# Attention stage of a decoder layer: the key projection's first step, two splits and a copy change places, and VectorE combines a long tile's probabilities in two parts

## The chip, the cores and the metric

The kernel runs on one core of one Trainium2 chip. The metric is the device time of one execution in microseconds (us), lower is better. TensorE multiplies, VectorE and ScalarE work on its results, GpSimd takes a few powers, SyncE and ScalarE issue the transfers.

## The reference, cut to what matters

One decoder layer over 1024 tokens of width 1024, in float32: an input projection, a chunked state scan (SSD), differential attention with four head pairs, an output projection, cross-attention into 256 memory tokens, and a squared-ReLU MLP, each with norms around it. What the change touches is above all the differential attention, and the first steps of the projection of the memory that comes next:

```python
def block(i):                                   # 128 queries, causal
    s = jnp.einsum('bhcqd,bhckd->bhcqk', qb, k) * scale
    p = jax.nn.softmax(jnp.where(causal, s, -jnp.inf), axis=-1)
    attn = p[:, :, 0] - lam * p[:, :, 1]
    return jnp.einsum('bhqk,bhkv->bhqv', attn, v)
...
k = (mem_h @ wk).reshape(B, M, MEM_HEADS, MEM_HEAD_DIM)
```

## The kernel before, in words

Each engine has its own hand-written list of instructions; semaphores tie the lists together. A float32 projection is made of three products, high by high, high by low and low by high (`three`, L2267 to L2269), so each weight half must be split into a high part by ScalarE (`split_hi`, L852) and a low part by VectorE (`split_lo`, L1452) before TensorE may use it. One weight unit is two halves.

**Before the attention** 64 projection steps (v, q, k, z; numbered n) run on TensorE, with the SSD chunks between them. At n = 32, the first step of k, VectorE does `ssd_first` (L1636 to L1638), then a rotary turn (`rope`, L1671 to L1675); at n = 33 it splits the second half of k's second unit, which TensorE needs for its next step. At n = 62 VectorE first splits the last half of the memory key's first unit and then makes the low part of the second memory tile (`tr_lo`, L1465); the first long scores wait for that tile's bank.

**The attention** has 32 steps: `ATT_STEPS` takes the query tiles in pairs, (3, 7), (2, 6), (1, 5), (0, 4), four heads each, a short tile (even step) and then a long one (odd step). Tile i has (i + 1) x 128 keys, so a short step has 128 to 512 and a long one 640 to 1024. For a step,
- TensorE makes the scores of both halves c (L2465, mask L2469). The next scores of the same kind need the two exponentials of the step two before.
- VectorE takes the row maxima (`attn_max`, L1746), ScalarE the exponentials (`attn_exp`, L1074), and VectorE then combines both halves (`attn_comb`: reciprocal L1753, ratio L1754, combination L1756).
- TensorE transposes the combined probabilities, four blocks of 128 keys at a time, into bank 6 (`probs_transpose`, L2479); ScalarE copies them out (`probs_evac`, L1088); a long step has a second part (blocks 4 to 7), for which bank 6 must have been copied out. Then TensorE multiplies with v (L2501) into one half of bank 7.

TensorE's list goes, for a pair: scores short, transposes short, values of the long step before, scores long, transposes long (part 0), values short, transposes long (part 1). VectorE's: max short c = 0, combination of the long step before, max short c = 1, max long c = 0, combination short, max long c = 1. Ahead of step 2's scores TensorE does 20 transposes of the identity (`KEEP`, L2486). The first two steps of the memory's key projection (mk, 24 products each) come at the end: step 0 after the values of the last long tile but one, step 1 after the last transposes, ahead of the last values. The weights of the steps after it (mk's second unit) are split in the same two places.

**The MLP's upper part**: TensorE runs through a list of products n; P1 products are copied to memory (`copy_p1`, L1334) before a P2 product may add to the same bank. ScalarE makes the high weights of product n + 5 (`quad_hi`, L1305), which may have to wait for their transfer, and copies P1 after that.

## Time and profile before

| what | value |
|---|---|
| time, median of 3 runs | 1426.94 us (1426.65 to 1427.15) |
| the profiled execution's own time | 1428.58 us |
| its span, first to last instruction | 1426.8 us, mean granted TensorE clock 0.997 |
| TensorE matmul busy | 1404.5 us (98%) |
| VectorE busy | 943.4 us (66%) |
| ScalarE busy | 665.9 us (47%) |
| chain that ended last | TensorE 90%, VectorE 3%, ScalarE 3% |

TensorE is busy for nearly the whole span. The span less its busy time is 22.3 us, so the idle stretches in front of TensorE's instructions are the places to look at; the attention stage, about 315 to 430 us from the start, holds most of those after the first load.

### The profile page before, as it was taken

What the parts mean: (1) busy time and instruction counts of PE and PEld (TensorE: products, weight loads), DVE (VectorE), ACT (ScalarE), POOL (GpSimd) and SP (SyncE); (2) the same over time, 40 slices, a digit from 0 to 9 for tenths busy, and PEclk for the clock granted to TensorE, in tenths of its full rate; (3) what the DMA queues carried; (4) which work ended last, traced back from release to release, by engine and by line L of the source; (5) the groups of instructions that cost most, each with busy time, mean ns of one, the idle gap of its engine ahead of it and who ended that gap; (6) DMA issues with size and microseconds to landing.
All of it is one profiled execution on the core that took longest, in us unless ns stands there. A gap on an engine that the chain in (4) does not pass through costs nothing.

```text
span 1426.8 us, 19458 instructions
## 1 busy us (share of the span) xinstructions
PE 1404.5 (98%) x7166; PEld 1175.2 (82%) x7166; DVE 943.4 (66%) x1516; ACT 665.9 (47%) x1296; POOL 70.7 (5%) x122
## 2 busy tenths in 40 slices
PE   9999999999989999999999999999999999999997
PEld 7889888876679888888888878888888888888886
DVE  4786577748868425444554888876666675467897
ACT  6225332347766325433433674444454654444443
POOL 0000000010002001010001200000000000000011
PEclk9999999999999999999999999999999999999999
DMA  9212233310004622221132325564442897776473
GB/s 325 70 39 75 82 103 90 101 70 16 1 16 148 221 59 104 75 59 59 60 119 79 128 97 181 201 223 161 156 151 111 291 354 253 226 236 193 154 233 129
DMA packets 98909, 194.45 MB, mean 136 GB/s; under 512 B 11200, under 2 KB 29696, under 8 KB 96768
## 3 DMA queue, kind: packets, MB, share of 16 engines
q1 hardware_dynamic: 87312, 153.30, 32.1%
q10 hardware_dynamic: 11504, 39.92, 8.5%
q8 instruction: 57, 0.93, 0.3%
q14 instruction: 36, 0.29, 0.1%
HBM read 147.01 MB, written 41.98 MB: 132 GB/s over the span
## 4 chain that ended last, share of the span: by engine, by line
PE 90%; DVE 3%; ACT 3%; issue 2%; DMA 2%; SPq 1%; ACTq 0%; POOLq 0%; POOL 0%; DVEq 0%
PE ps L2267 27%; PE ps L2269 27%; PE ps L2268 27%; PE ps L2465 2%; PE ps L2501 2%; PE ps L2479 1%; PE ps L2407 1%; PE ps L2331 1%; DMA x_in<-in_x_dram 1%; PE ps L2410 1%; ACT junk L857 0%; ACT probs L1074 0%; PE ps L2623 0%; PE ps L2415 0%; SPq L612 0%
## 5 line engine op out<-in xcount | busy, mean ns | idle before, releaser
L2267 PE MATMUL ps<-d_ring 128*128 128x512 f32 x448 | 174.3, 389 | 0.0
L2268 PE MATMUL ps<-d_ring 128*128 128x512 f32 x448 | 174.3, 389 | 0.0
L2269 PE MATMUL ps<-d_ring 128*128 128x512 f32 x448 | 174.3, 389 | 0.0
L2267 PE MATMUL ps<-wh,oph 128*128 128x512 f32 (+1 forms) x448 | 162.5, 363 | 0.9 <-DVE wl L1448 0.9
L2269 PE MATMUL ps<-wh,opl 128*128 128x512 f32 (+1 forms) x448 | 161.0, 359 | 0.0
L2268 PE MATMUL ps<-wl,oph 128*128 128x512 f32 (+1 forms) x448 | 160.4, 358 | 0.0
L2267 PE MATMUL ps<-oph,wh 128*128 128x512 f32 x384 | 152.2, 396 | 1.7 <-DVE opl L1483 0.9
L2269 PE MATMUL ps<-oph,wl 128*128 128x512 f32 x384 | 149.6, 390 | 0.0
L2268 PE MATMUL ps<-opl,wh 128*128 128x512 f32 x384 | 149.5, 389 | 0.0
L1372 ACT ACTIVATE d_ring<-left_raw 128x512 fp32r<-128x512 f32 x112 | 70.2, 627 | 92.7 <-PE ps L2269 76.9
L2115 DVE TENSOR_TENSOR d_ring<-left_raw,d_ring 128x512 fp32r<-128x512 f32 x112 | 78.2, 698 | 52.4 <-ACT d_ring L1372 52.2
L797 POOL TENSOR_TENSOR rms<-stat,mhalf 128x1 f32<-128x1 f32 (+2 forms) x59 | 57.3, 974 | 1096.7 <-DVE stat L1456 1074.9
L2267 PE MATMUL ps<-oph,wq_h 128*128 128x512 f32 x256 | 100.1, 391 | 1.5 <-ACT p_s L1334 1.5
L2269 PE MATMUL ps<-oph,wq_l 128*128 128x512 f32 x256 | 99.7, 389 | 0.0
L2268 PE MATMUL ps<-opl,wq_h 128*128 128x512 f32 x256 | 99.6, 389 | 0.0
L2268 PEld LDWEIGHTS ps<-d_ring 128*128 128x128 f32 x448 | 84.1, 188 | 17.6
L2269 PEld LDWEIGHTS ps<-d_ring 128*128 128x128 f32 x448 | 84.1, 188 | 17.4
L2267 PEld LDWEIGHTS ps<-d_ring 128*128 128x128 f32 x448 | 84.1, 188 | 17.4
L2267 PEld LDWEIGHTS ps<-wh,oph 128*128 128x128 f32 x448 | 84.2, 188 | 13.4 <-issue 1.1
L2269 PEld LDWEIGHTS ps<-wh,opl 128*128 128x128 f32 x448 | 84.1, 188 | 12.6
L2268 PEld LDWEIGHTS ps<-wl,oph 128*128 128x128 f32 x448 | 84.3, 188 | 11.8
L2267 PEld LDWEIGHTS ps<-oph,wh 128*128 128x128 f32 x384 | 72.1, 188 | 17.4 <-DVE opl L1483 1.7
(347 smaller groups left out, 2907.6 us busy)
## 6 DMA issues: line engine op xcount, KB each, us to landing
right_raw<-in_w_down_dram SPq DMA_DIRECT2D x128, 256.0 KB, 3.8
u_kept_s<-us SPq DMA_DIRECT2D x64, 256.0 KB, 3.3
left_raw<-u_kept_s SPq DMA_DIRECT2D x64, 256.0 KB, 2.8
w_blk<-in_w_up_blocks_dram ACTq DMA_DIRECT2D x14, 1024.0 KB, 5.8
left_raw<-u_kept_a SPq DMA_DIRECT2D x48, 256.0 KB, 3.1
raw<-in_w_in_dram SPq DMA_DIRECT2D x16, 512.0 KB, 4.2
u_kept_a<-u SPq DMA_DIRECT2D x24, 256.0 KB, 2.4
x_in<-in_x_dram SPq DMA_DIRECT2D x8, 512.0 KB, 9.1
```

The source lines that it names most:

```text
L797: g.tensor_tensor(dst, src, mhalf[:, 0:w], ALU.pow).then_inc(rms_ready, 1)
L1372: s.activation(d_ring[m % DRING][:, 0, :], left_raw[:, m % 4, :], ACT.Copy).then_inc(dn_hi, 1)
L2115: v.tensor_tensor(ring[:, 1, :], left_raw[:, m % 4, :], ring[:, 0, :].bitcast(F32), ALU.subtract).then_inc(dn_lo, 1)
L2267: te.matmul(o, lh, rh, start=first, stop=False, skip_group_check=more)
L2268: te.matmul(o, lh, rl, start=False, stop=False, skip_group_check=more)
L2269: return te.matmul(o, ll, rh, start=False, stop=last, skip_group_check=more)
L2331: ins = te.transpose(ps[:, tr_bank(n, b), k * P:(k + 1) * P], src(4 * b + k), ident[:])
L2407: te.matmul(ps[:, 4, h * 64:(h + 1) * 64], cb_decay[:, h, :], xdt[:, h * 64:(h + 1) * 64], start=True, stop=True)
L2410: ins = te.matmul(ps[:, 6, gr * 256:(gr + 1) * 256], b_cb[:, gr, :], xdt_end[:, gr * 256:(gr + 1) * 256], start=True, stop=True)
L2465: te.matmul(ps[:, score_bank(i, c) + k0 // 512, 0:kn], qt[half, h, i * P:(i + 1) * P], kt[half, h, k0:k0 + kn], start=True, stop=not diag)
L2479: ins = te.transpose(ps[:, 6, (b % 4) * P:(b % 4 + 1) * P], probs[:, k % 2, 0, b * P:(b + 1) * P], ident[:])
L2501: ins = te.matmul(o, probs_t[:, k % 2, b, :], vt[:, b, h * P:(h + 1) * P], start=b == 0, stop=b == i)
```

## The change

Eight edits, all in the lists of instructions.
1. At n = 32 VectorE splits k's next half directly after `ssd_first`, ahead of the rotary turn.
2. At n = 62 the low part of the second memory tile comes ahead of the weight split.
3. mk's step 0 (24 products) takes the place of the 20 identity transposes at step 2. It goes to the upper half of bank 7, which ScalarE copies to a small buffer (`kmt_first`) between the exponentials of step 1; later one copy brings it to its place. For that the squares of tiles 6 and 7 of y go to memory in place of bank 7.
4. VectorE takes both maxima of step 1 before it combines step 0.
5. The combination of a long step is two instructions, keys 0 to 511 and the rest, each with its own event; the transposes of blocks 0 to 3 wait for the first only.
6. The second part of a long step of tile 4 or 5 (one or two blocks) is transposed into the upper half of bank 7, so it doesn't wait for bank 6 to be copied out.
7. At the end only mk's step 1 is left, ahead of the last short tile's last work; the halves of mk's second unit are split earlier (ScalarE's first at step 0, the others at step 32).
8. For the P1 products of blocks 4 to 7 `copy_p1` comes ahead of `quad_hi`.

```diff
                 act.wait_ge(gate_done, i + 1)
-                square(("y", i), mix[:, 0:4, i * P:(i + 1) * P], ps[:, 7, :].rearrange("p (k c) -> p k c", k=4))
+                dst = o_part[i - 6][:] if i >= 6 else ps[:, 7, :].rearrange("p (k c) -> p k c", k=4)
+                square(("y", i), mix[:, 0:4, i * P:(i + 1) * P], dst)
...
                 if n >= 2:
-                    act.wait_ge(comb_done, n - 1) if c else act.wait_ge(pt_done, PT_END[n - 2])
+                    act.wait_ge(comb_done if c else pt_done, PT_END[n - 2])
                 b = score_bank(steps[n][0], c)
...
                 nb = min(4, i + 1 - 4 * part)
-                s.activation(probs_t[:, k % 2, 4 * part:4 * part + nb, :].rearrange("p b k -> p (b k)"), ps[:, 6, 0:nb * P],
+                src = ps[:, 7, 2 * P:(2 + nb) * P] if part and nb <= 2 else ps[:, 6, 0:nb * P]
+                s.activation(probs_t[:, k % 2, 4 * part:4 * part + nb, :].rearrange("p b k -> p (b k)"), src,
                              ACT.Copy).then_inc(pt_ev, 1)
...
                     probs_evac(n - 2, 1)
+                if n == 0:
+                    split_hi(2 * UNIT0["mk"] + 2)
                 if n < NS:
                     attn_exp(n, 0)
+                if n == 1:
+                    act.wait_ge(pj_done, STEP0["mk"] + 1)
+                    s.activation(kmt_first[:], ps[:, 7, MEM:2 * MEM], ACT.Copy).then_inc(ev["mk"], 1)
+                if n < NS:
                     attn_exp(n, 1)
...
                     act.dma_start(gain_a[:], rows(t["norm_mix_post"][0:1, :])).then_inc(gain_a_loaded, 16)
-                if n in (NS, NS + 1):
-                    for q in split_at("mk", n - NS):
-                        split_hi(q)
+                if n == NS:
+                    split_hi(2 * UNIT0["mk"] + 3)
...
                         split_hi(q)
+                if n == 0:
+                    act.wait_ge(ev["mk"], 1)
+                    after(s.activation(kmt[:, 0, :], kmt_first[:], ACT.Copy))
+                    continue
                 act.wait_ge(pj_done, g + 1)
...
                 b, p = UP[n]
+                if p == "P1" and NP <= n < 2 * NP:
+                    copy_p1(b)
                 if n + LEAD + 1 < len(UP):
...
                     u_square(n)
-                if p == "P1":
+                if p == "P1" and not NP <= n < 2 * NP:
                     copy_p1(b)
...
                     v.tensor_tensor(y, y, silu_z[:, i % 2, :].rearrange("p (k c) -> p k c", k=4), ALU.mult).then_inc(gate_done, 1)
-                for q in split_at(name, st):
-                    split_lo(q)
+                if n == MEM_TR + MT + 1:
+                    tr_lo(TR_MEM + MT - 1, memh[:, :, (MT - 1) * P:MT * P], meml[:, :, (MT - 1) * P:MT * P])
+                if n != LO_SOON + 1:
+                    for q in split_at(name, st):
+                        split_lo(q)
                 if 1 <= n < 5:
...
                     ssd_first(SSD_FIRST[n])
+                if n == LO_SOON:
+                    for q in split_at(name, st + 1):
+                        split_lo(q)
                 if n in SSD_MID:
...
                     normalise(("mem", i), TR_MEM + i, h_mem[:, i, :], gain_b[:], h_mem[:, i, :])
-                if 0 <= n - MEM_TR - 2 < MT:
+                if 0 <= n - MEM_TR - 2 < MT - 1:
                     i = n - MEM_TR - 2
...
                                              lam[:, 4:5], ALU.mult, ALU.mult))
-                v.scalar_tensor_tensor(probs[:, n % 2, 0, 0:keys], probs[:, n % 2, 1, 0:keys], ratio[:, n % 2:n % 2 + 1],
-                                       probs[:, n % 2, 0, 0:keys], ALU.mult, ALU.add).then_inc(comb_done, 1)
+                for cut in (slice(0, min(keys, 512)), slice(512, keys)):
+                    if cut.start < cut.stop:
+                        v.scalar_tensor_tensor(probs[:, n % 2, 0, cut], probs[:, n % 2, 1, cut], ratio[:, n % 2:n % 2 + 1],
+                                               probs[:, n % 2, 0, cut], ALU.mult, ALU.add).then_inc(comb_done, 1)
...
                     attn_max(n, 0)
-                if 1 <= n <= NS:
+                if 2 <= n <= NS:
                     attn_comb(n - 1)
...
                     attn_max(n, 1)
+                if n == 1:
+                    attn_comb(0)
                 if n in (0, 2, 3):
...
                     y_mean(5 + n)
-                if n in (NS, NS + 1):
-                    for q in split_at("mk", n - NS):
-                        split_lo(q)
+                if n == NS:
+                    for half in range(2):
+                        split_lo(2 * UNIT0["mk"] + 2 + half)
                 if n == NS + 1:
...
-            def feature_step(name, st, rh, rl, f, c0, n, unit=None, middle=None):
+            def feature_step(name, st, rh, rl, f, c0, n, unit=None, middle=None, place=None):
...
                 g, u = STEP0[name] + st, UNIT0[name] + (st // per if unit is None else unit)
-                bank_free(pe, g)
+                if place is None:
+                    bank_free(pe, g)
+                    place = ps[:, bank(g), 0:n]
                 unit_ready(u)
...
                         pe.wait_ge(xt_lo, KD + k + 1)
-                    ins = three(ps[:, bank(g), 0:n], wcols(wh, u % 2, k, f * P, P), wcols(wl, u % 2, k, f * P, P),
+                    ins = three(place, wcols(wh, u % 2, k, f * P, P), wcols(wl, u % 2, k, f * P, P),
                                 rh[:, k, c0:c0 + n], rl[:, k, c0:c0 + n], k == 0, k == KD - 1)
...
                 m = PT_AT[(k, part)]
-                pe.wait_ge(comb_done, k + 1)
+                nb = min(4, i + 1 - 4 * part)
+                beside = part and nb <= 2
+                pe.wait_ge(comb_done, m + 1)
                 if m:
-                    pe.wait_ge(pt_ev, m)
-                for b in range(4 * part, min(4 * part + 4, i + 1)):
-                    ins = te.transpose(ps[:, 6, (b % 4) * P:(b % 4 + 1) * P],
+                    pe.wait_ge(pt_ev, m - 1 if beside else m)
+                for b in range(4 * part, 4 * part + nb):
+                    ins = te.transpose(ps[:, 7, (2 + b % 4) * P:(3 + b % 4) * P] if beside else ps[:, 6, (b % 4) * P:(b % 4 + 1) * P],
                                        probs[:, k % 2, 0, b * P:(b + 1) * P], ident[:])
...
                 if n == 2:
-                    for _ in range(KEEP):
-                        te.transpose(ps[:, 6, 0:P], ident[:], ident[:])
+                    pe.wait_ge(sq_done, SQ[("y", 5)] + 1)
+                    feature_step("mk", 0, memh, meml, 0, 0, MEM, place=ps[:, 7, MEM:2 * MEM])
                 if n < NS:
...
                     i, h = steps[k]
-                    if k == 0:
-                        pe.wait_ge(sq_done, SQ[("y", NT - 1)] + 1)
                     pe.wait_ge(pt_ev, PT_END[k])
...
                     probs_transpose(n - 2, 1)
-                if n in (NS, NS + 1):
+                if n == NS:
                     for c in range(2):
                         pe.wait_ge(ex_done[c], NS)
-                    feature_step("mk", n - NS, memh, meml, n - NS, 0, MEM)
+                    feature_step("mk", 1, memh, meml, 1, 0, MEM)
```

VectorE at the start of the attention, before: `nmax` is a row maximum, `recs` and `ratio` lead to the combination, which is `probs<-probs,ratio`; `stat` and `mix` belong to y's norms.

```order
L1746 TENSOR_REDUCE nmax<-ps 128x1
L1753 RECIPROCAL recs<-sums 128x2
L1754 SCALAR_TENSOR_TENSOR ratio<-sums,recs,lam 128x1
L1756 SCALAR_TENSOR_TENSOR probs<-probs,ratio 128x512
L1746 TENSOR_REDUCE nmax<-ps 128x1
L1456 TENSOR_SCALAR stat<-stat 128x1
L1746 TENSOR_REDUCE nmax<-ps 128x1
L1753 RECIPROCAL recs<-sums 128x2
L1754 SCALAR_TENSOR_TENSOR ratio<-sums,recs,lam 128x1
L1756 SCALAR_TENSOR_TENSOR probs<-probs,ratio 128x1024
```

The same place on VectorE now, with the changed kernel's line numbers:

```order
L1766 TENSOR_REDUCE nmax<-ps 128x1 x2
L1773 RECIPROCAL recs<-sums 128x2
L1774 SCALAR_TENSOR_TENSOR ratio<-sums,recs,lam 128x1
L1778 SCALAR_TENSOR_TENSOR probs<-probs,ratio 128x512
L1470 TENSOR_SCALAR stat<-stat 128x1
L1766 TENSOR_REDUCE nmax<-ps 128x1
L1773 RECIPROCAL recs<-sums 128x2
L1774 SCALAR_TENSOR_TENSOR ratio<-sums,recs,lam 128x1
L1778 SCALAR_TENSOR_TENSOR probs<-probs,ratio 128x512 x2
```

Both maxima of step 1 now stand ahead of step 0's combination, and step 1's combination of 1024 keys has become two of 512.

TensorE at the same place before: scores of step 1 (`kt,qt` x4) and mask, the identity transposes, scores of step 2, transposes of step 0.

```order
L2465 MATMUL ps<-kt,qt 128x512 x4
L2469 MATMUL ps<-mask_q,ident_b 128x128 x2
L2486 MATMUL ps<-ident 128x128 x20
L2465 MATMUL ps<-kt,qt 128x512 x2
L2469 MATMUL ps<-mask_q,ident_b 128x128 x2
L2479 MATMUL ps<-ident,probs 128x128 x4
```

TensorE there now; `memh`, `meml` are the memory's high and low parts, `wh`, `wl` the weights', and the three rows of mk's step 0 come eight times.

```order
L2491 MATMUL ps<-kt,qt 128x512 x4
L2495 MATMUL ps<-mask_q,ident_b 128x128 x2
L2291 MATMUL ps<-memh,wh 128x256
L2292 MATMUL ps<-meml,wh 128x256
L2293 MATMUL ps<-memh,wl 128x256
...
L2491 MATMUL ps<-kt,qt 128x512 x2
L2495 MATMUL ps<-mask_q,ident_b 128x128 x2
```

The 24 products stand where the 20 transposes stood.

TensorE at the end of the attention before: the last transposes (one block of the last long step), mk's step 1, the last values (`vt,probs_t`) behind it.

```order
L2479 MATMUL ps<-ident,probs 128x128 x4
L2501 MATMUL ps<-vt,probs_t 128x128
L2479 MATMUL ps<-ident,probs 128x128
L2267 MATMUL ps<-memh,wh 128x256
L2268 MATMUL ps<-meml,wh 128x256
```

And now:

```order
L2507 MATMUL ps<-ident,probs 128x128 x4
L2527 MATMUL ps<-vt,probs_t 128x128
L2507 MATMUL ps<-ident,probs 128x128
L2527 MATMUL ps<-vt,probs_t 128x128 x5
L2291 MATMUL ps<-memh,wh 128x256
```

The last values follow the last transposes at once; one of the two mk steps that stood around them has gone to the start, the other stands ahead of these rows.

## Rows read from the trace of the kernel before

**Rows 1.** The page: busy time, share and instructions of each engine.

```profile
PE 1404.5 (98%) x7166; PEld 1175.2 (82%) x7166; DVE 943.4 (66%) x1516; ACT 665.9 (47%) x1296; POOL 70.7 (5%) x122
```

**Rows 2.** Timeline, second half of k's unit: start, length, instruction, [idle before it].

```profile
212.80 0.68 DVE L1638 TENSOR_TENSOR x_skip<-ps,heads 128x512 f32<-128x512 f32 x1
...
215.33 1.22 DVE L1452 TENSOR_TENSOR wl<-raw,wh 128x1024 fp32r<-128x1024 f32 x1
...
216.61 0.50 PE L2267 MATMUL ps<-oph,wh 128*128 128x512 f32 x1 [0.79 <-DVE wl L1452]
```

**Rows 3.** Timeline, the first steps of the attention.

```profile
317.29 1.99 PE L2465 MATMUL ps<-kt,qt 64*128 64x512 f32 x8 [0.86 <-DVE meml L1465]
...
319.33 2.35 PE L2486 MATMUL ps<-ident 128*128 128x128 f32 x20
...
323.02 1.22 DVE L1746 TENSOR_REDUCE nmax<-ps 128x1 f32<-128x1024 f32 x1
323.16 0.66 PE L2479 MATMUL ps<-ident,probs 128*128 128x128 f32 x4 [0.20 <-DVE probs L1756]
...
324.27 1.11 ACT L1074 ACTIVATE probs<-ps,nmax 128x1024 f32<-128x1024 f32 x1 [1.04 <-DVE nmax L1746]
...
325.62 3.18 PE L2465 MATMUL ps<-kt,qt 64*128 64x512 f32 x8 [1.81 <-ACT probs L1074]
```

**Rows 4.** Half a microsecond of that: TensorE's busy time and count, granted clock, DMA.

```profile
327.00:327.50 0.50, 0.50 (x4) 0.50 0.20 66
```

**Rows 5.** Timeline, two steps of the pairs (3, 7).

```profile
334.24 0.17 DVE L1753 RECIPROCAL recs<-sums 128x2 f32<-128x2 f32 x1 [0.71 <-ACT probs L1074]
...
334.70 1.28 DVE L1756 SCALAR_TENSOR_TENSOR probs<-probs,ratio 128x1024 f32<-128x1024 f32 x1
334.75 1.99 PE L2465 MATMUL ps<-kt,qt 64*128 64x512 f32 x8
...
335.90 0.68 DVE L1746 TENSOR_REDUCE nmax<-ps 128x1 f32<-128x512 f32 x1
...
338.18 0.63 PE L2479 MATMUL ps<-ident,probs 128*128 128x128 f32 x4
...
338.52 0.75 DVE L1756 SCALAR_TENSOR_TENSOR probs<-probs,ratio 128x512 f32<-128x512 f32 x1
...
339.19 1.81 DVE L1746 TENSOR_REDUCE nmax<-ps 128x1 f32<-128x1024 f32 x2
...
341.75 0.17 DVE L1753 RECIPROCAL recs<-sums 128x2 f32<-128x2 f32 x1 [0.74 <-ACT probs L1074]
```

**Rows 6.** Timeline, one step of the pairs (1, 5).

```profile
391.15 0.41 PE L2479 MATMUL ps<-ident,probs 128*128 128x128 f32 x2 [0.33 <-ACT probs_t L1088]
...
391.62 1.28 DVE L1746 TENSOR_REDUCE nmax<-ps 128x1 f32<-128x768 f32 x2
...
392.75 0.90 ACT L1074 ACTIVATE probs<-ps,nmax 128x768 f32<-128x768 f32 x1
```

**Rows 7.** Timeline, one step of the pairs (0, 4).

```profile
413.00 0.30 PE L2479 MATMUL ps<-ident,probs 128*128 128x128 f32 x1 [0.56 <-ACT probs_t L1088]
```

**Rows 8.** Timeline, the end of the attention.

```profile
424.68 0.30 PE L2479 MATMUL ps<-ident,probs 128*128 128x128 f32 x1 [0.56 <-ACT probs_t L1088]
425.01 0.28 ACT L1088 ACTIVATE probs_t<-ps 128x128 f32<-128x128 f32 x1
...
427.86 1.28 PE L2501 MATMUL ps<-vt,probs_t 128*128 128x128 f32 x10
...
429.66 0.36 PE L2267 MATMUL ps<-memh,wh 128*128 128x256 f32 x1 [0.52 <-issue]
```

**Rows 9.** Timeline, the MLP's upper part, products 8 to 10.

```profile
834.46 0.63 ACT L1305 ACTIVATE wq_h<-w_half_t 128x512 fp32r<-128x512 f32 x1 [3.42 <-DMA w_half_t<-in_w_up_blocks_dram]
...
836.55 0.57 ACT L1334 ACTIVATE p_s<-ps 128x512 f32<-128x512 f32 x1
...
837.27 0.47 PE L2267 MATMUL ps<-oph,wq_h 128*128 128x512 f32 x1 [1.23 <-ACT p_s L1334]
```

More of the change, by code:

```diff
@@ L47 @@
 WARM = 40
-KEEP = 20
 LAMBDA_INIT = 0.8 - 0.6 * math.exp(-0.3 * 0)
@@ L197 @@
 ROPE_SOON = {n + 2: x for n, x in ROPE_AT.items() if x[2] == 2 * NT - 3}
+LO_SOON = 32
 GATE_AT = {48 + n: QKZ_STEPS[n][1] for n in QKZ_EVENT}
@@ L332, in build @@
         vmt = at("vmt", "V", 8192, [P, KD, MEM])
+        kmt_first = at("kmt_first", "TMP", 13312, [P, MEM])
         kmh = at("kmh", "GA", 0, [P, KD, MEM], F32R)
@@ L1097, in o_square @@
                 else:
-                    act.wait_ge(sq_done, 2 * NT)
+                    act.wait_ge(sq_done, SQ[("y", NT - 1)] + 1)
                 s.activation(o_part[m % 2][:], mix[:, 4:8, i * P:(i + 1) * P], ACT.Square).then_inc(o_sq, 1)
```

## Prediction

> **What bounds the kernel now.** I began with the engines' busy times [rows 1]: TensorE is busy for 1404.5 of 1426.8 us. A change can win only the 22.3 us in which TensorE stands still, or work that it takes off TensorE. So I next read what TensorE waited for, place by place, with the timeline around each place that an edit touches.
> - In k's second unit TensorE waits 0.79 us for a low half on VectorE [rows 2].
> - At the attention's start it waits 0.86 us for `meml`, and 1.81 us for step 1's second exponential; the scores behind that wait take 3.18 us [rows 3], where the same 8 matmuls take 1.99 us in the steady part [rows 5]. The granted clock there is 0.50, the 1.2 GHz level [rows 4].
> - In the pairs (3, 7) no TensorE row shows a wait [rows 5]. In the pairs (1, 5) and (0, 4) the second transposes wait 0.33 and 0.56 us for the copy out of bank 6 [rows 6, 7].
> - At the end two mk steps and 0.52 us of idle time stand around the last values [rows 8]. In the MLP one copy holds TensorE for 1.23 us [rows 9].
>
> **The change part by part.** Minus is faster.
>
> *A, k's split (edit 1).* `x_skip` ends at 213.48, and the split follows at 215.33 with 1.22 us [rows 2]. The split now starts about 1.9 us sooner and ends near 214.7, before TensorE has run out of work at 216.61 − 0.79 = 215.82. **−0.79.** Behind it the rotary turn comes 1.2 us later and its own readers wait; no row shows TensorE waiting for them, so I bound the loss by what is left if half comes back: −0.4 to −0.8.
>
> *B, the start (edits 2 to 4).* Three things change places. `meml` before the split frees the first long scores' bank, so TensorE passes 317.29 up to 0.86 us sooner [rows 3]. mk's step 0 costs 2.9 us at full clock: the same 24 products lie between 424.98 (424.68 + 0.30) and 427.86 [rows 8]. The transposes that it replaces took 2.35 [rows 3]. So it ends at about 319.33 − 0.86 + 2.9, that is 321.4, near where the transposes ended (321.68): nothing is lost on TensorE, and 2.9 us of work that was needed anyway now lie where only filling stood. If the 0.86 doesn't come, it ends 0.6 later; the next scores then start 0.6 later, but the transposes behind them wait for VectorE anyhow. Next, step 1's second maximum (323.02, 1.22 us [rows 3]) goes ahead of step 0's combination, which with its reciprocal took 0.46 + 0.67 ahead of it (as 338.52 to 339.19 and 334.24 to 334.70 in [rows 5]): it starts near 321.9 and is done at 323.1. The exponential comes behind it and behind the copy to `kmt_first` (about 0.4, by the 0.28 for 128 columns in [rows 8]), so near 323.5, where before it started at 324.27. Step 0's combination is what is late instead: it ends near 323.1 + 0.46 + 0.75 = 324.3, its transposes (0.66) start there instead of at 323.16, and TensorE comes to the next long scores at 325.0 instead of 325.62. Against that, those scores and what follows may run at full clock, since TensorE now stands still for one stretch of about 1.4 us (it was through at 323.16 − 0.20 = 322.96 before) instead of 0.20 and 1.81. The chain: step 1's reciprocal comes some 1.4 us behind that exponential's start (its 1.11 and the sum), at 324.9; a steady cycle of 7.51 (334.24 to 341.75 [rows 5]) lengthened by the 0.14 below gives the next at 332.55, where before it came at 334.24: 1.7 us sooner. VectorE's norms of y lie in that stretch too, so I take **−1.4**; bounds 0 and −1.9.
>
> *C, the split combination in tiles 7 and 6 (edit 5).* In the pairs (3, 7) the reciprocal comes 0.46 ahead of the combination, which starts at 334.70; the next maximum starts 1.20 later, at 335.90. From it 2.28 lead to the second transposes at 338.18 (exponential and copy on ScalarE), and 3.57 from there to the next reciprocal (copy, two exponentials): 0.46 + 1.20 + 2.28 + 3.57 = 7.51 [rows 5], the period itself. I see no slack in that ring, though TensorE has no wait in it either: its own work and the ring are equally long. A combination of 512 keys takes 0.67 to the next start (338.52 to 339.19), so two take 1.34 where one took 1.20: 0.14 per long step. What it gives: the first four blocks could be transposed 0.6 us sooner. But TensorE comes to them only after its scores, at 334.75 + 1.99 = 336.74, and the whole combination was done at 334.70 + 1.28 = 335.98. So the gain is nothing there and the cost stands: eight long steps of these tiles, seven cycles between them, **+0.98**. Bounds: 0, if TensorE's own work is what sets the period, and 1.1 for all eight. The Trainium skill, VectorE: DVE Perf Modes, section "The TRN2 errata — SBUF-src ops pay a fixed extra latency per instruction", speaks against such a cut: the latency is paid once for a large tile and again for each small one. Its figure of 151 cycles at 0.96 GHz is, as an estimate, 0.157 us; the rows agree with 0.14.
>
> *D, the second transposes beside (edit 6).* These waits of 0.33 and 0.56 us [rows 6, 7], seven of them between two cycles, have no cause any more. TensorE doesn't keep all of it, since VectorE's path is next: in the pairs (1, 5) the first of two maxima of 768 keys starts at 391.62 and takes about 0.9 (1.22 for 1024 in [rows 3]), so it is done at 392.5, and the exponential that needs it starts at 392.75 [rows 6]: 0.2 spare, of which the two-part combination takes 0.14. I take 0.06 for each of seven: **−0.42**; for the pairs (0, 4) I read no other spare and take the same. Bounds: 0, and 7 × 0.2 = −1.4, if the split costs nothing here.
>
> *E, the end (edits 3, 7).* Of the two mk steps one is gone, −2.9 (B). The other no longer hides the last copy: before, it ran between the last transposes and the last values; now the values follow the transposes and wait for a copy of 0.28 [rows 8] and its hand-over, about 0.5. The 0.56 in front of the transposes goes, but the mk step that now precedes them was not waiting for anything either. **−2.4**, bounds −2.0 and −2.9. The 0.52 behind the values I leave as it is.
>
> *F, `copy_p1` (edit 8).* ScalarE stood from 831.04 to 834.46 for the transfer of a weight, and the copy came behind that at 836.55 [rows 9]. Put ahead, it needs only its products, two of which lie before 836.04 (837.27 − 1.23); it is done while TensorE works, and the weight is rounded when it arrives. **−1.23**; the bound on the other side is −0.8, if ScalarE then has the weight ready later.
>
> Sum: −0.79 − 1.4 + 0.98 − 0.42 − 2.4 − 1.23 = −5.26. The profiled execution's own time is 1428.58, 1.8 above its span, so it would be 1423.3; it lies 1.64 above the median of the runs, 1426.94, and by that median the forecast is **1421.7 us**.
>
> **The rivals.**
> - *The split is free.* TensorE shows no wait in the pairs (3, 7), and VectorE stands still for 0.71 us before the reciprocal [rows 5]. If that is room, C is 0 and D reaches about −0.9: −5.26 − 0.98 − 0.5 = −6.7, **1420.2**. Against it: the 0.71 is a wait for ScalarE within the ring, whose four links add up to the period.
> - *The split is paid on all sixteen long steps*, since each has one instruction more: 16 × 0.14 = 2.24 for C and D together instead of 0.98 − 0.42: −3.6, **1423.4**. The section of the Trainium skill named above would have it so: 16 × 0.157 = 2.5 as an estimate. For it: no spare of 0.2 is sure. Against it: TensorE's waits in [rows 6, 7] are larger than 0.14, and go.
> - *The start gains nothing*: the clock falls as before, and the exponential moves forward only as far as the copy and step 0's combination move back. B is 0: −3.9, **1423.1**.
> - *The dummy work was needed* (the other side). The 20 transposes filled an idle stretch, and now TensorE stands still 1.4 us in one piece. Where the clock falls to 0.50, eight matmuls cost 3.18 instead of 1.99, 1.2 us a time [rows 3 to 5]. From the seventh further fall, (5.26 + 2.85) / 1.2, the kernel is measurably slower, about **1430**. For it: the fall came just behind idle time. Against it: one fall stood in this whole stretch before, mk's 24 products fill the place, and the later waits shrink.
> - *The edits do little*: A, B and D all miss, leaving C, E and F: 0.98 − 2.4 − 1.23 = −2.65, **1424.3**.
>
> **How the numbers follow.** Forecast 0.52, free split 0.16, split paid everywhere 0.08, start without gain 0.13, little 0.08, clock 0.03. The predicted time is that of the first. The range runs from the free split with E at its bound (1420.2 − 0.5) to the little case, **1419.6 to 1424.4**; what lies outside is the clock's case and a part of the two outer ones, about 0.15. A measurement of this kernel tells about 0.2%, 2.85 us, from no change, so faster means below 1424.09. All of the first four cases lie there, but with their bounds a few hundredths of the third and fourth don't: faster 0.85, same 0.12, slower 0.03.
>
> **What the profile of the changed kernel would show.** A: no wait for `wl` near 216. B: no wait for `meml`, 24 products where the transposes were, step 1's second exponential near 323.5, step 3's scores 1.99 long and a clock of 1.00 behind them; a 0.50 there would refute it. C: two combinations 0.67 apart and a period of 7.65 in the pairs (3, 7); 7.50 would mean that the split is free. D: no wait of the second transposes, and pairs shorter by less than 0.1; shorter by 0.3 or more would mean that VectorE was not next. E: values about 0.5 us behind the last transposes, and mk's second unit at once behind them. F: no wait for `p_s` at product 10. The forecast is wrong if a wait in front of TensorE that isn't in these rows takes one of these places: that of mk's step 0 for its second half's weights, for instance, whose split VectorE now does last before the attention.

## The result and the profile after

The changed kernel takes **1420.09 us** (median of 4 runs, 1419.74 to 1420.69), the kernel before beside it 1427.05 (4 runs, 1426.65 to 1427.31): 6.96 us less. The ratio of the paired runs is 0.9947 with an interval of 0.9935 to 0.9959. Against the 1426.94 us that it was worked out from, the forecast of 1421.7 us is a ratio of 0.9963, outside that interval; the range's fast end, 1419.6, is 0.9949, and the measured ratio lies just beyond it, though 1420.09 us itself is inside the range. The direction was right; the gain is a third larger than forecast.

The page of the changed kernel begins with its span and the engines' busy times:

```profile
span 1418.1 us, 19434 instructions
...
PE 1400.1 (99%) x7146; PEld 1172.8 (83%) x7146; DVE 944.8 (67%) x1532; ACT 666.0 (47%) x1297; POOL 70.6 (5%) x122
```

The span is 8.7 us shorter than in the trace before and TensorE is busy 4.4 us less [rows 1]; its idle time fell from 22.3 to 18.0 us. The list of TensorE's waits in the changed kernel, over the whole span (in all, times, longest):

```profile
PE ps L2507 <- DVE probs L1778: 2.6, 4, 1.4
...
PE ps L2491 <- ACT probs L1076: 1.2, 5, 0.3
...
PE ps L2527 <- ACT probs_t L1091: 1.0, 1, 1.0
PE ps L2507 <- ACT probs_t L1091: 0.9, 4, 0.3
```

The waits for `wl`, for `meml` and of 1.23 us for `p_s` are gone. Three are new: short tiles' transposes that wait for VectorE (1.45 at the start, 0.80 at the end), long scores that wait for an exponential (five times, at most 0.30), and the last values, 1.04 us.

To see where the time went, I cut the span at the same instructions of TensorE in three traces: the one shown ahead of the prediction, a later one of the same kernel (its run took 1426.83 us), and the one of the changed kernel (1419.81).

| stretch, between starts on TensorE | before, first trace | before, third trace | changed | forecast of the difference |
|---|---|---|---|---|
| start to the first short scores | 315.08 | 315.26 | 314.26 | −0.79 (A) |
| to the third long scores | 19.67 | 18.35 | 17.71 | −1.4 (B) |
| seven cycles, tiles 7 and 6, to the tenth | 47.64 | 47.66 | 48.13 | +0.98 (C) |
| six cycles, tiles 5 and 4, to the sixteenth | 32.92 | 32.92 | 31.66 | −0.42 (D, for seven) |
| to mk's second unit | 14.35 | 14.36 | 11.66 | −2.4 (E) |
| to the output projection | 48.37 | 47.76 | 47.27 | 0 |
| to the MLP's lower part | 636.80 | 636.79 | 635.38 | −1.23 (F) |
| to the end | 311.99 | 311.99 | 311.99 | 0 |

The first trace before holds 1.9 us that the third doesn't, in the second row (a fall of the clock) and the sixth. Against the third the differences are −1.00, −0.64, +0.47, −1.26, −2.70, −0.49, −1.41 and 0.00, together −7.0, close to the difference of the medians. So the gain beyond the forecast lies in C, D, the end and the sixth stretch, not in one place, and B came out smaller than forecast.

The timeline of VectorE in the changed kernel where k's half is split:

```profile
213.12 0.68 DVE L1652 TENSOR_TENSOR x_skip<-ps,heads 128x512 f32<-128x512 f32 x1
213.72 1.21 DVE L1466 TENSOR_TENSOR wl<-raw,wh 128x1024 fp32r<-128x1024 f32 x1
```

And of all engines at the attention's start:

```profile
319.96 2.35 DVE L1766 TENSOR_REDUCE nmax<-ps 128x1 f32<-128x1024 f32 x2
...
322.32 0.38 ACT L1124 ACTIVATE kmt_first<-ps 128x256 f32<-128x256 f32 x1
...
322.58 1.12 ACT L1076 ACTIVATE probs<-ps,nmax 128x1024 f32<-128x1024 f32 x1
...
323.48 0.66 PE L2507 MATMUL ps<-ident,probs 128*128 128x128 f32 x4 [1.45 <-DVE probs L1778]
...
324.06 1.99 PE L2491 MATMUL ps<-kt,qt 64*128 64x512 f32 x8
```

The split follows `x_skip` at once, and no product waits for it [rows 2]. At the start both maxima run as one group at 319.96; the exponential starts at 322.58, where before it was 324.27; the short transposes wait 1.45 us for the combination, as worked out; and the long scores behind them follow without a wait and take 1.99 us, where [rows 3] had 1.81 and 3.18. The granted clock, third from last in a row of the windows, is 1.00 where [rows 4] has 0.50:

```profile
327.00:328.00 1.00, 0.70 (x7) 0.54 (x6) 1.00 (x2) 0.76 (x3) 0.54 (x1) 1.00 0.00 0
```

The timeline of a pair (3, 7) in the changed kernel:

```profile
331.97 1.99 PE L2491 MATMUL ps<-kt,qt 64*128 64x512 f32 x8
...
332.09 1.42 DVE L1778 SCALAR_TENSOR_TENSOR probs<-probs,ratio 128x512 f32<-128x512 f32 x2
...
333.42 1.96 DVE L1766 TENSOR_REDUCE nmax<-ps 128x1 f32<-128x512 f32 x2
...
334.14 0.69 ACT L1076 ACTIVATE probs<-ps,nmax 128x512 f32<-128x512 f32 x1 [1.01 <-DVE nmax L1766]
...
334.73 0.19 ACT L1076 ACTIVATION_READ_ACCUMULATOR probs<-ps,nmax 128x1 f32 x1
334.82 0.59 ACT L1091 ACTIVATE probs_t<-ps 128x512 f32<-128x512 f32 x1
...
335.55 0.63 PE L2507 MATMUL ps<-ident,probs 128*128 128x128 f32 x4
```

And of a pair (0, 4):

```profile
406.87 1.35 PE L2491 MATMUL ps<-kt,qt 64*128 64x512 f32 x8 [0.30 <-ACT probs L1076]
...
408.22 1.03 DVE L1766 TENSOR_REDUCE nmax<-ps 128x1 f32<-128x128 f32 x2
...
409.16 0.15 DVE L1773 RECIPROCAL recs<-sums 128x2 f32<-128x2 f32 x1
```

In the first the two parts of the combination take 1.33 to the next start (333.42 − 332.09), 0.13 more than the 1.20 of [rows 5], where 0.14 was forecast, and the second transposes lie 3.58 behind the scores (335.55 − 331.97), where [rows 5] has 3.43 (338.18 − 334.75). In the second no transposes wait for a copy any more [rows 7]. The long scores now wait for an exponential, 0.30 us.

The timeline of the attention's end in the changed kernel:

```profile
420.18 0.60 ACT L1091 ACTIVATE probs_t<-ps 128x512 f32<-128x512 f32 x1 [1.77 <-PE ps L2507]
...
420.68 0.62 ACT L1102 ACTIVATE o_part<-mix 128x512 f32<-128x512 f32 x1
...
421.19 0.27 ACT L1091 ACTIVATE probs_t<-ps 128x128 f32<-128x128 f32 x1
...
421.52 1.38 PE L2527 MATMUL ps<-vt,probs_t 128*128 128x128 f32 x10 [1.04 <-ACT probs_t L1091]
```

mk's step between the last transposes and the last values is gone [rows 8], and the values wait 1.04 us, not the 0.5 that I had set: ScalarE squares an output tile between the two copies.

### The profile page after: what moved, and what is told of

The parts are those of the page before. It is cut to its first block, busy times and chain, and to the rows that moved or that the text cites. A ratio compares the mean times of both kernels' runs of the same rounds, so it can differ in the third digit from the quotient of the medians.

```text
span 1418.1 us, 19434 instructions
## 1 busy us (share of the span) xinstructions
PE 1400.1 (99%) x7146; PEld 1172.8 (83%) x7146; DVE 944.8 (67%) x1532; ACT 666.0 (47%) x1297; POOL 70.6 (5%) x122
## 4 chain that ended last, share of the span: by engine, by line
PE 90%; DVE 3%; ACT 2%; issue 2%; DMA 1%; SPq 1%; POOL 0%; POOLq 0%; DVEq 0%; ACTq 0%
PE ps L2291 27%; PE ps L2293 27%; PE ps L2292 27%; PE ps L2491 1%; PE ps L2527 1%; PE ps L2357 1%; PE ps L2433 1%; DMA x_in<-in_x_dram 1%; DVE nmax L1766 1%; PE ps L2507 1%; ACT probs L1076 1%; PE ps L2436 1%; ACT junk L858 0%; PE ps L2649 0%; PE ps L2441 0%
```

## The experiments

**The kernel before, twice more.** No edit; to see what of its first trace belongs to the kernel.

> The kernel before again. In its first trace TensorE waits 0.93 us at 478.03 for a low half of the output projection's weights, and that execution took 1428.58 where the median is 1426.94. If that wait belongs to the kernel it stands again (0.9), and the changed kernel, which has no such wait, won it by an edit. If it is a matter of one execution it is gone or under 0.3, with a time near 1426.9. The stages of the attention (47.64, 32.92, and 14.35 from the last long scores to mk's second unit) within 0.1 either way; one clock fall to 0.50 near 327.

> The kernel before a third time, for two things that differed between its traces. The clock behind the wait of 1.81: if it falls in some executions only, either 0.50 with scores of about 3 us, or 1.00 with 1.99, and the third long scores 19.6 or 18.35 behind the first short ones. The wait of 0.9 at the output projection's weights: it stood in both traces of this kernel, in none of the changed one, but in neither of the kernel before with one edit alone; if it belongs to the kernel it stands here too, if it is a matter of the execution it may be gone.

The runs took 1427.78 and 1426.83 us. In both traces step 3's scores take 1.99 us at a clock of 1.00, behind the same wait. TensorE's timeline in the third trace:

```profile
325.81 1.99 PE L2465 MATMUL ps<-kt,qt 64*128 64x512 f32 x8 [1.81 <-ACT probs L1074]
```

So the fall of the clock, 1.3 us, comes in some executions of this kernel only. The wait at the output projection was 0.87 in the second trace and is missing in the third: its going is no work of an edit. Without it that stretch takes 47.76 here, and 47.25 to 47.40 in all variants of the changed kernel. In the third trace ScalarE still waits 0.45 us for the transfer of these weights before it can split them:

```profile
473.38 1.34 ACT L849 ACTIVATE wh<-raw,gain_o 128x512 fp32r<-128x512 f32 x2 [0.45 <-DMA raw<-in_w_out_dram]
```

In the changed kernel the same row comes without such a wait.

**Only the order of the start undone.** The changed kernel with step 0's combination first again:

```diff
-                if 2 <= n <= NS:
+                if 1 <= n <= NS:
                     attn_comb(n - 1)
...
-                if n == 1:
-                    attn_comb(0)
```

> The changed kernel with step 0's combination ahead of step 1's second maximum again. Theory A (one idle stretch of TensorE instead of two with 1.81 us just ahead of the long scores is what keeps the clock): step 3's scores start about 324.0 to 324.4, wait about 1.5 us, granted clock 0.50 behind them, they take 3.18 us, and the next long scores start about 1.2 us later than in the changed kernel (331.97), at 333.2. Theory B (mk's products ahead of it keep the clock): the scores take 1.99 us, granted clock 1.00, next long scores within 0.4 us of 331.97.

Time 1421.61 us. The wait of 1.81 is back, and the clock fell; the third long scores start 19.62 behind the first short ones, 1.9 later than in the changed kernel. TensorE's timeline there:

```profile
324.89 3.06 PE L2489 MATMUL ps<-kt,qt 64*128 64x512 f32 x8 [1.81 <-ACT probs L1076]
```

Its windows, the granted clock third from last:

```profile
326.00:327.00 1.00, 1.00 (x6) 0.38 (x2) 1.00 (x3) 0.51 (x2) 0.00 (x0) 0.50 0.18 70
```

**Only the order of the start changed**, in the kernel before:

```diff
-                if 1 <= n <= NS:
+                if 2 <= n <= NS:
                     attn_comb(n - 1)
...
+                if n == 1:
+                    attn_comb(0)
```

> The kernel before with both maxima of step 1 ahead of step 0's combination, nothing else. If this order alone brings the start's gain: step 3's scores without a wait of 1.8, their length 1.99, granted clock 1.00 behind them, third long scores 17.7 to 17.9 behind the first short ones (before: 19.67 with the clock's fall and 18.35 without; changed kernel: 17.71). If mk's products and the earlier tile of the memory are needed for it: 18.3 or more.

Time 1426.11 us. TensorE's timeline at the same place:

```profile
324.64 0.66 PE L2481 MATMUL ps<-ident,probs 128*128 128x128 f32 x4 [1.33 <-DVE probs L1756]
325.23 1.99 PE L2467 MATMUL ps<-kt,qt 64*128 64x512 f32 x8
```

One wait of 1.33 us, no wait ahead of the scores, a clock of 1.00 behind them, and 17.57 us to the third long scores: the order alone brings the whole of the start's gain, with the 20 dummy transposes in place. Over all traces: of six with the wait of 1.81 the clock fell in three (the first trace before, the order undone, the cut alone below) and not in the other three; in none of the seven with the new order. Five of the six, two with the fall and three without, have the same rows on TensorE ahead of the wait; the order undone has mk's products there. The Trainium skill, TensorE: Matmul & The Clock Gate, section "What's actually happening", has the clock follow how busy TensorE was shortly before. The traces agree in so far as the fall came only behind that idle time; but the same rows with the same wait were followed by either clock, so the rows alone don't tell which.

**The combination in one piece again**, in the changed kernel.

```diff
...
-                for cut in (slice(0, min(keys, 512)), slice(512, keys)):
+                for cut in (slice(0, keys),):
...
-                pe.wait_ge(comb_done, m + 1)
+                pe.wait_ge(comb_done, k + 1)
```

> The changed kernel with the long tiles' combination in one instruction again, all else kept. Stages by the starts of long scores: from the third long step's to the tenth's (seven cycles, tiles 7 and 6) 47.64 us before and 48.13 in the changed kernel; from the tenth's to the last's (tiles 5 and 4) 32.92 and 31.66. Theory of the prediction (the combination closes a ring in tiles 7 and 6 and costs 0.14 a cycle): 48.13 - 0.98 = 47.15, and 31.66 - 6 x 0.14 = 30.8, the whole kernel 1.8 us faster than the changed one (about 1418.3). Rival 1 (in tiles 7 and 6 the copy waits for the first four blocks' transposes, which come at TensorE's pace, so that VectorE had some 0.13 to spare): 47.64 as before and no shorter, then 30.8, about 1.3 us faster (1418.8). Rival 2 (the early first half is what lets the other edits gain): tiles 5 and 4 take longer than 31.66, the kernel is not faster than 1420.1.

Time 1418.98 us (5 runs, 1418.59 to 1419.31), ratio to the kernel before 0.9938 (0.9925 to 0.9950). Seven cycles of tiles 7 and 6 take 47.65, exactly as before the change, six of tiles 5 and 4 take 31.52. So the cut costs 0.48 and 0.14, not 0.98 and 0.84, and another 0.13 ahead of the third long scores (17.57 here, from the first short ones). For tiles 7 and 6 the first rival had the time right; the 30.8 that both theories had for tiles 5 and 4 was wrong. This kernel's timeline shows why, in two cycles of the pairs (3, 7):

```profile
331.49 1.99 PE L2491 MATMUL ps<-kt,qt 64*128 64x512 f32 x8
...
333.53 0.61 PE L2507 MATMUL ps<-ident,probs 128*128 128x128 f32 x4
...
334.12 0.19 ACT L1076 ACTIVATION_READ_ACCUMULATOR probs<-ps,nmax 128x1 f32 x1
334.21 0.59 ACT L1091 ACTIVATE probs_t<-ps 128x512 f32<-128x512 f32 x1
...
334.94 0.63 PE L2507 MATMUL ps<-ident,probs 128*128 128x128 f32 x4
...
339.01 1.99 PE L2491 MATMUL ps<-kt,qt 64*128 64x512 f32 x8
...
341.05 0.61 PE L2507 MATMUL ps<-ident,probs 128*128 128x128 f32 x4
...
341.45 0.19 ACT L1076 ACTIVATION_READ_ACCUMULATOR probs<-ps,nmax 128x1 f32 x1
...
341.69 0.60 ACT L1091 ACTIVATE probs_t<-ps 128x512 f32<-128x512 f32 x1
...
342.43 0.63 PE L2507 MATMUL ps<-ident,probs 128*128 128x128 f32 x4
```

In the second of them ScalarE reads the accumulator at 341.45 and could copy 0.09 later, as it does at 334.73 and 334.82 in the changed kernel. It copies at 341.69, when the first transposes (341.05 + 0.61) are done. Those come at TensorE's pace, behind the long scores. VectorE's chain, which leads to the read, had some 0.15 us to spare at this link. In the first cycle it had none: the copy at 334.21 follows the read at 334.12 by those 0.09, and the transposes were done before. There the changed kernel's copy comes 0.13 later behind the scores (2.85 for 2.72), and so do its second transposes (3.58 for 3.45).

The same can be read in each of the seven cycles. The spare time is the copy's start in this kernel, less the read's start and 0.09:

| cycle | 1 | 2 | 3 | 4 | 5 | 6 | 7 |
|---|---|---|---|---|---|---|---|
| spare, combination in one piece | 0 | 0.15 | 0 | 0.20 | 0.08 | 0.08 | 0 |
| cost of the cut | 0.12 | 0 | 0.13 | 0 | 0.05 | 0.05 | 0.13 |

The cut makes VectorE 0.13 later, and costs what of that the spare time doesn't cover. In three cycles VectorE's chain comes last at this link, and there the prediction's reading holds; in the others TensorE's transposes do. The same kernel's timeline in a pair (0, 4):

```profile
405.78 1.35 PE L2491 MATMUL ps<-kt,qt 64*128 64x512 f32 x8 [0.30 <-ACT probs L1076]
...
406.99 1.16 DVE L1766 TENSOR_REDUCE nmax<-ps 128x1 f32<-128x128 f32 x2
...
407.06 0.29 PE L2495 MATMUL ps<-mask_q,ident_b 128*128 128x128 bf16 x2
...
408.07 0.15 DVE L1773 RECIPROCAL recs<-sums 128x2 f32<-128x2 f32 x1
```

The two maxima take 1.16 together here and 1.03 behind the cut combination; the short reciprocal comes 2.29 behind the long scores in both (408.07 − 405.78, 409.16 − 406.87). The second maximum is that of the long scores and waits for their mask (407.06), so the combination lies beside TensorE's scores, and the cut is hidden there.

**The combination in three pieces**, in the changed kernel.

```diff
-                for cut in (slice(0, min(keys, 512)), slice(512, keys)):
+                for cut in (slice(0, 256), slice(256, 512), slice(512, keys)) if keys > 512 else (slice(0, keys),):
...
+                        if cut.stop in (512, keys):
+                            ins.then_inc(comb_done, 1)
```

> The changed kernel with the combination of a long tile in three instructions (keys 0 to 255, 256 to 511, the rest), transposes released as before the cut. Theory of the first four transposes (VectorE had some 0.07 to 0.13 of room per cycle in tiles 7 and 6 and the cut in two has used it): every further instruction costs its full 0.14: seven cycles at 48.13 + 0.98 = 49.1, six cycles of tiles 5 and 4 at 31.66 + 0.5 to 0.84 = 32.2 to 32.5. Rival (an instruction more costs only the 0.07 that the cut in two cost on the average, 0.48 in seven cycles): 48.6 and 31.8.

Time 1421.62 us; 48.94 and 32.32. The third instruction costs 0.81 in seven cycles and 0.66 in six, 0.11 to 0.12 each: close to its full price, now that the room is used. It is cheapest, 0.06, in the fourth cycle, where the cut in two had left some room. The Trainium skill's fixed latency per instruction, 0.157 us as an estimate (VectorE: DVE Perf Modes, section "The TRN2 errata — SBUF-src ops pay a fixed extra latency per instruction"), agrees with VectorE's own time, 0.13 for the first cut; but the kernel paid that only in the cycles without spare time, and half of it or less on the average.

**The cut alone**, in the kernel before:

```diff
...
-                v.scalar_tensor_tensor(probs[:, n % 2, 0, 0:keys], probs[:, n % 2, 1, 0:keys], ratio[:, n % 2:n % 2 + 1],
+                for cut in (slice(0, min(keys, 512)), slice(512, keys)):
...
-                pe.wait_ge(comb_done, k + 1)
+                pe.wait_ge(comb_done, m + 1)
```

> The kernel before with the cut combination alone. Ring theory of the prediction: seven cycles of tiles 7 and 6 at 47.64 + 0.98 = 48.62. First-four-transposes theory: 48.13, as in the changed kernel. In tiles 5 and 4, where the second transposes still wait for the copy out of bank 6: 32.92 + 0.84 = 33.8 if VectorE's path leads to that copy, 32.9 if the first transposes do. Wait at the output projection's weights (0.9) still there if it hangs on mk's place.

Time 1428.46 us; 47.96 and 33.10: +0.32 and +0.18. Neither theory had the 47.96. The clock fell at its start, which leaves TensorE behind VectorE as the cycles begin: the third long scores start 0.05 behind the combination, where in the changed kernel they start 0.12 ahead of it. So the first cycle has room for the cut here, and takes 7.49 as in the first trace before (7.50). The run with the order undone has the cut and the fall too, and also takes 47.96. Cutting bought nothing in any kernel. The wait at the output projection was missing here and in the run with the order alone.

**The second transposes beside, alone**, in the kernel before.

```diff
...
-                if m:
-                    pe.wait_ge(pt_ev, m)
-                for b in range(4 * part, min(4 * part + 4, i + 1)):
-                    ins = te.transpose(ps[:, 6, (b % 4) * P:(b % 4 + 1) * P],
+                nb = min(4, i + 1 - 4 * part)
+                beside = part and nb <= 2
+                if m:
+                    pe.wait_ge(pt_ev, m - 1 if beside else m)
+                for b in range(4 * part, 4 * part + nb):
+                    ins = te.transpose(ps[:, 7, (2 + b % 4) * P:(3 + b % 4) * P] if beside else ps[:, 6, (b % 4) * P:(b % 4 + 1) * P],
...
```

> The kernel before with edit 6 alone: the second transposes of tiles 5 and 4 beside bank 6, the combination in one piece. If the ring of the long scores (scores, mask, maximum, short combination, maximum, exponential, next long scores) is what is next behind the bank, and the combination lies beside it: six cycles of tiles 5 and 4 at 31.5, as in the changed kernel with one combination, 1.4 less than before (32.92), and long scores waiting 0.2 to 0.3 for an exponential. By the prediction's reading (0.2 to spare on VectorE at each): 32.92 - 1.2 = 31.7 without the cut, 32.5 with it. Tiles 7 and 6 unchanged at 47.64.

Time 1425.23 us. Six cycles take 31.52, the same hundredth as the changed kernel with one combination, and the end is 1.14 shorter (13.22); tiles 7 and 6 stay as they were (47.66). This kernel's list of TensorE's waits between the attention's start and its end:

```profile
PE ps L2465 <- ACT probs L1074: 3.0, 6, 1.8
PE ps L2481 <- DVE probs L1756: 1.1, 3, 0.8
PE ps L2481 <- ACT probs_t L1088: 0.4, 2, 0.2
```

Of the first, 1.81 is that of the start; the other five are long scores that wait 0.20 to 0.30 for an exponential. That is the ring that comes next: long scores, mask, maximum, short combination, the long tile's second maximum, exponential, next long scores.

**`copy_p1` behind again**, in the changed kernel.

```diff
-                if p == "P1" and NP <= n < 2 * NP:
-                    copy_p1(b)
...
-                if p == "P1" and not NP <= n < 2 * NP:
+                if p == "P1":
```

> The changed kernel with the copy of P1 behind the weight's rounding again for all products. By the prediction's term: TensorE waits 1.2 us for the copy at product 10 again, and from the memory's transposes to the first product of the MLP's lower part it takes 1.2 us more than in the changed kernel (442.2). If the stage's gain of 1.45 has another part beside the wait: 1.45 more.

Time 1421.04 us. The wait is back at the same product, in this kernel's timeline:

```profile
829.04 0.58 ACT L1346 ACTIVATE p_s<-ps 128x512 f32<-128x512 f32 x1
...
829.76 0.47 PE L2289 MATMUL ps<-oph,wq_h 128*128 128x512 f32 x1 [1.35 <-ACT p_s L1346]
```

From the memory's transposes to the MLP's lower part it takes 443.81 for 442.19, 1.62 more, of which 1.35 are this wait.

**The last square behind the last copy**, in the changed kernel.

```diff
-                if n in (NS, NS + 1):
-                    o_square(n - NS)
+                if n == NS:
+                    o_square(0)
...
                     probs_evac(n - 2, 1)
+                if n == NS + 1:
+                    o_square(1)
```

> The changed kernel with the square of the last output tile but one (0.62 us on ScalarE) behind the copy of the last transposes instead of ahead of it. In the changed kernel the last values wait 1.04 us for that copy. If the square is what makes it late: the copy at 420.7 instead of 421.2, the last values at 421.07 instead of 421.52, wait 0.6, mk's second unit 0.45 earlier, the kernel 0.45 us faster. Rival: VectorE's mean of that tile, which waits for the square, and the norms behind it hold the next steps instead: mk's second unit 0.45 earlier, but the time comes back as a wait before 475 us and the kernel's time is unchanged.

Time 1419.07 us (5 runs, 1418.84 to 1419.67). The last values wait half as long, and the end takes 11.14 for 11.66. This kernel's timeline:

```profile
419.84 0.77 ACT L1091 ACTIVATE probs_t<-ps 128x512 f32<-128x512 f32 x2 [1.77 <-PE ps L2509]
...
420.49 0.63 ACT L1102 ACTIVATE o_part<-mix 128x512 f32<-128x512 f32 x1
...
420.65 1.38 PE L2529 MATMUL ps<-vt,probs_t 128*128 128x128 f32 x10 [0.52 <-ACT probs_t L1091]
```

Of the 0.52 some 0.4 are kept: the output projection comes 47.40 behind mk's second unit, 0.13 later than in the changed kernel, and the later stretches are as long as there.

**Both**, one combination and the later square.

> The changed kernel with the combination in one instruction and the last square behind the last copy. The two gains lie in different stages, so they should add: seven cycles of tiles 7 and 6 at 47.65, six of tiles 5 and 4 at 31.52, 11.14 from the last long scores to mk's second unit; 0.5 us below the kernel with the single combination alone, near 1418.4. If the square's 0.5 comes back as a wait further on: 1418.9.

Time 1418.63 us (5 runs, 1418.19 to 1419.44), ratio 0.9940 (0.9926 to 0.9954); 47.65, 31.52 and 11.15. The stages add as expected, less 0.10 at the output projection (47.35, for 47.25 with one combination alone). By the medians it is the fastest kernel here, 1.5 us below the changed one. The 0.35 below the single combination alone lies inside the spread of the runs, the two ratios to the kernel before (0.9940 and 0.9938) don't tell them apart, and only the stage shows it.

## Why the prediction was wrong, step by step

*A* held, and was sized somewhat low. No row waits for the split. Forecast were −0.79; the first short scores start 0.82 and 1.00 earlier than in two traces before, but the 215 us ahead of the split differ by up to 0.6 between executions. From the last product ahead of the split to those scores it takes 98.53 in all seven traces with the edit and 99.65 to 99.98 in the six without: at least 1.12. The 0.79 is idle time behind a matmul's modelled end; by the starts the waiting product comes 0.95 earlier (1.18 behind the product ahead of it before, 0.23 now).

*B*: the mechanism held, the size depends on what it is held against. Exponential (322.58), transposes (323.48) and scores (324.06) came where the working put them, each 0.8 to 0.9 earlier by A's gain. Where I took −1.4, it is −1.96 against the trace that I worked from, and −0.64 against one whose clock didn't fall. I took the fall for a part of the kernel; it is one of its outcomes. The sum then took the −1.4 from the median of the runs, though the trace that it was worked out from lies 1.64 above that median. mk's 24 products took no part in this stretch's gain: the order alone gave all of it. So the rival *the start gains nothing* is refuted too.

*C* is the first step that failed: "I see no slack in that ring". The four links run from one reciprocal to the next, so they add up to the period whatever slack they hold; the sum proved nothing. One of them, the 2.28 from the maximum to the second transposes, held a wait of some 0.15 us on ScalarE for the first transposes. [rows 5] has no row of ScalarE. Its timeline in the same trace shows no idle time there either, because it was reading an accumulator for part of it; it could have copied 0.09 behind 337.20, as above:

```profile
337.20 0.19 ACT L1074 ACTIVATION_READ_ACCUMULATOR probs<-ps,nmax 128x1 f32 x1
337.44 0.60 ACT L1088 ACTIVATE probs_t<-ps 128x512 f32<-128x512 f32 x1
```

Nor was one cycle good for all seven: in that trace they take 7.50, 7.28, 7.01, 6.62, 6.62, 6.42 and 6.19, and the spare time differs from cycle to cycle, as in the table above. +0.48 in place of +0.98.

*D* is the second, and the larger: "0.2 spare, of which the two-part combination takes 0.14". The spare was near the right size (by the run with edit 6 alone the cycles are shorter by 0.14 to 0.16 in the pairs (1, 5), 0.22 in the pairs (0, 4), and 0.52 at the step from one to the other; for the pairs (0, 4) I had no row, and that 0.2 is near there is luck), but the cut takes nearly none of it, since the combination lies beside the long scores. I had charged 0.14 seven times to a path on which it hardly stands. −1.26 in six cycles in place of −0.42; without the cut −1.40.

*E*: −2.70 in place of −2.4. Two errors nearly cancel, which is luck. Edit 6 removes two waits of 0.56 inside this stretch, 1.14 by the run with edit 6 alone, for which D had 0.06 and E nothing. The rest, 1.56 (13.22 to 11.66), is what moving mk's step brought with the other edits, above all because the wait for the last copy is 1.04, not 0.5: the square lies between the copies. Another 0.2 to 0.5, in a stretch for which the sum had nothing, appear between mk's second unit and the output projection (47.25 to 47.40 in every variant of the changed kernel, 47.59 to 47.76 where nothing waited there in the kernel before and its variants). A shorter wait of ScalarE for the transfer of the output projection's weights goes with it; which edit brings it wasn't tried.

*F*: −1.41 against −1.23, the wait itself and a little more; by the run that undoes it 1.62.

Of the rivals, "the split is free" was nearest, with 1420.2 beside 1420.09, but for another reason than TensorE's missing waits in the pairs (3, 7): the cut costs 0.75 in all, by the run with one combination, and the ends of D and E make up for it. "Paid on all sixteen" and "little" are refuted by the stages, and the clock never fell in the changed order.

## What to carry to other kernels

Links from one event to its next occurrence always add up to the period, so the sum doesn't prove a ring: look in each link for the instruction that started later than its engine and its visible input allowed, and ask which other engine's pace it follows, in more than one cycle. Before charging a cost to a path, ask whether the costly instruction stands on it; here one that was paid in some pairs lay beside the scores in others. And take a second trace of the kernel before: what differs between two executions of the same kernel, here 1.3 us of clock and 0.9 us of a load, is no gain of an edit.

## What the runs showed of the hardware

The granted clock's fall to 0.50 behind the wait of 1.81 us came in three of six traces, in two of the five with the same rows on TensorE ahead of it, and cost 1.2 to 1.3 us there: the third long scores 19.58 and 19.67 behind the first short ones, for 18.35. One idle stretch of 1.33 to 1.46 us was never followed by a fall, in seven traces. What decides it between equal traces stays open.
